# Attention with tokens held by grid columns, half of the keys for the neighbourhood heads, and bias tables stored and read in larger pieces

## The reference

```
h = HybridMixer(x)     # one q/k/v projection; 8 differential heads (each the difference of two softmaxes
                       # over all 512 keys, with a T5 relative bias); 8 neighbourhood heads; output projection
x = LayerNorm(alpha * x + h)
f = PEER(x)            # 8 heads pick 16 of 128*128 single-neuron experts per token
x = LayerNorm(alpha * x + f)
```

```
col_start = jnp.clip(c - NA_WIN_W // 2, 0, GRID_W - NA_WIN_W)
in_win = (c[None, :] >= col_start[:, None]) & (c[None, :] < col_start[:, None] + NA_WIN_W)
bias = jnp.where(in_win[None, None, :, None, :], bias, NEG_INF)
```

## Time and profile before

| | |
|---|---|
| median of 3 runs | 3465.18 us (3463.68 to 3468.54) |
| profiled execution | 3473.33 us, span 3471.5 us |
| mean granted clock of TensorE | 0.964 |
| PE busy | 3242.8 us, 93% of the span |
| DVE busy | 2541.5 us, 73% |
| ACT busy | 1238.2 us, 36% |
| POOL busy | 882.0 us, 25% |

### The profile page before, as it was taken

One profiled execution on the slowest core, in us unless ns is written; L12 is line 12 of the kernel. 1 busy time (PEld: TensorE's weight loads), 2 busy tenths in 40 slices (PEclk: granted clock), 3 DMA queues, 4 the chain that ended last, 5 costly groups with the idle time before them and its releaser, 6 DMA issues. The chain is left out here.

```text
span 3471.5 us, 49403 instructions
## 1 busy us (share of the span) xinstructions
PE 3242.8 (93%) x17110; PEld 2854.6 (82%) x17110; DVE 2541.5 (73%) x5172; ACT 1238.2 (36%) x1716; POOL 882.0 (25%) x624
## 2 busy tenths in 40 slices
PE   6989799899999999999879887998999999999997
PEld 5966589899899999988658665898998999999886
DVE  2166478999688878878721764789996888787787
ACT  2255333344333333333322642333443333333332
POOL 0030001100255545433200200011002555454332
PEclk8989899999999999999989898999999999999999
DMA  7541224445899999989675412244468999998896
GB/s 246 160 113 64 88 85 135 169 181 226 302 356 338 349 328 340 319 308 350 222 229 154 135 39 99 74 146 158 181 236 318 341 362 347 311 343 311 316 350 226
DMA packets 361706, 811.60 MB, mean 234 GB/s; under 512 B 51246, under 2 KB 222766, under 8 KB 327246
## 3 DMA queue, kind: packets, MB, share of 16 engines
q1 hardware_dynamic: 287822, 541.22, 45.5%
q0 software_dynamic: 73728, 268.47, 20.7%
HBM read 718.38 MB, written 99.09 MB: 235 GB/s over the span
## 5 line engine op out<-in xcount | busy, mean ns | idle before, releaser
L221 PE MATMUL o_bank<-v_hi,w_hi 128*128 128x512 f32 x1536 | 599.6, 390 | 10.2 <-DVE w_lo L1526 10.2
L222 PE MATMUL o_bank<-v_lo,w_hi 128*128 128x512 f32 x1536 | 600.6, 391 | 0.0
L223 PE MATMUL o_bank<-v_hi,w_lo 128*128 128x512 f32 x1536 | 600.4, 391 | 0.0
L158 POOL DMA_INDIRECT g_ring<-in_peer_u,g_idx x256 | 363.8, 1421 | 794.0 <-DVE g_ring L168 743.6
L158 POOL DMA_INDIRECT g_ring<-in_peer_v,g_idx x256 | 369.8, 1445 | 508.4 <-DVE x_sb L176 453.9
L221 PE MATMUL h_bank<-x_hi,ws_hi 128*128 128x384 f32 x1152 | 387.1, 336 | 4.5 <-PEq L1194 4.5
L223 PE MATMUL h_bank<-x_hi,ws_lo 128*128 128x384 f32 x1152 | 387.0, 336 | 0.0
L222 PE MATMUL h_bank<-x_lo,ws_hi 128*128 128x384 f32 x1152 | 386.7, 336 | 0.0
L1511 DVE TENSOR_TENSOR v_lo<-v_raw,v_hi 128x2048 fp32r<-128x2048 f32 x128 | 292.9, 2288 | 124.9 <-ACT v_hi L1446 123.0
L168 DVE SCALAR_TENSOR_TENSOR g_ring<-g_ring,x_sb 128x1024 f32<-128x1024 f32 x256 | 306.4, 1222 | 97.8 <-DMA g_ring<-in_peer_u,g_idx 97.3
L176 DVE SCALAR_TENSOR_TENSOR x_sb<-g_ring,g_h,x_sb 128x1024 f32<-128x1024 f32 x256 | 328.4, 1283 | 56.1 <-DMA g_ring<-in_peer_v,g_idx 37.7
(11 more groups left out here) (187 smaller groups left out, 6014.8 us busy)
## 6 DMA issues: line engine op xcount, KB each, us to landing
ws_raw<-in_uT SPq DMA_DIRECT2D x128, 1024.0 KB
v_raw<-in_peer_v SPq DMA_DIRECT2D x128, 1024.0 KB
gates_T<-gate_stage SPq DMA_DIRECT2D x12, 4096.0 KB, 12.6
g_raw<-gates_T SPq DMA_DIRECT2D x128, 384.0 KB
w_raw<-in_w_in SPq DMA_DIRECT2D x24, 1024.0 KB, 7.4
ws_raw<-hidden_T SPq DMA_DIRECT2D x56, 384.0 KB
w_out_half<-in_w_out SPq DMA_DIRECT2D x8, 2048.0 KB, 7.9
ws_raw<-in_peer_wq SPq DMA_DIRECT2D x16, 1024.0 KB
```

The costliest lines, as they stand in the source:

```text
L158: nc.gpsimd.indirect_dma_start(out=tail.ring[n % RING][:, :], out_offset=None, in_=table.rearrange("l e d -> (l e) d"), in_offset=bass.Ind ...
L221: nc.tensor.matmul(out, lh, rh, start=start, stop=False)
L222: nc.tensor.matmul(out, lh, rl, start=False, stop=False)
L223: return nc.tensor.matmul(out, ll, rh, start=False, stop=stop)
```

## The change

The tokens of a tile are now 16 grid columns with all 8 rows of each (`column_tokens`), so the window of a tile's queries lies in 32 columns, 256 keys (`NKEYS`), whose first column depends on the tile (`FIRST_COL`). Neighbourhood heads make, exponentiate, transpose and multiply 256 keys where they did 512. For tiles 1 and 2 the keys begin in the middle of a v tile, so `nv2` is a copy of v shifted by 64 partitions. `x` and the output are loaded and stored in four transfers each.

The bias tables keep their order by rows, and `maxima` reads them with a view that puts columns first (`rearrange("p (r c) -> p c r")`), so that the step between two numbers read is 64 (`tb`) or 32 (`nb`). `tb` has 560 numbers per head and partition where it had 896. The table of the neighbourhood heads is loaded raw (8 x 48 numbers per head) into the buffer of `w_out`, in 8 transfers; GpSimd adds one of three masks and writes the result to `nb`, first for the left edge (8 instructions of 256 numbers), then for the middle and the right edge (8 of 512). SyncE waits for all ten signals (`nb_ready`) before it loads `w_out`.

The 2-D bias is copied to DRAM in 128 rows of 30720 bytes (before: 7680 of 512); the T5 vectors are stored once, in `setup`, from ScalarE's queue. Tail pieces have other slots, the RMS norm has semaphores of its own, and `read_diff` waits for the projection of the tile before (`hid`). In `route` VectorE keeps 3 splits and GpSimd does the other 22, in front of the `place_off` of each head.

```
-TBW = T + (TT - 1) * P
+TC = GW // TT
+TBW = T + (TT - 1) * TC
 DRS = 2 * WIN_H - 1
-RPW = 2 * GW
-NBR = 2 * GR - 2
+RPW = GW
+KC = TC + WIN_W
+NKEYS = KC * GR
+FIRST_COL = (0, TC - WIN_W // 2, 2 * TC - WIN_W // 2, GW - KC)
+EDGE = (0, 1, 1, 2)
+SPAN = KC + TC
+RPL = TC
+RPC = NNH * DRS * RPW + GR * RPW
...
+def column_tokens(t, n):
+
+    return at(t, n * TC * D, [[D, TC], [GW * D, GR], [1, D]])
...
+            act.wait_ge(vec_made, 2)
+            nc.scalar.dma_start(at(t5_scratch, 0, [[NDH * REL, P], [REL, NDH], [1, REL]]),
+                                per["t5_vec"][:, None, :].to_broadcast([P, NDH, REL])).then_inc(t5_stored, 16)
...
-            sp.dma_start(rpb_scratch, at(a["na_rpb"], l * (NNH * DRS * RPW), [[RPW, NNH * DRS], [0, GW], [1, RPW]]))\
+            sp.dma_start(at(rpb_scratch, 0, [[GR * RPC + 1, TC], [RPC + RPW, GR], [1, NNH * DRS * RPW]]),
+                         at(a["na_rpb"], l * (NNH * DRS * RPW), [[0, TC], [0, GR], [1, NNH * DRS * RPW]]))\
                 .then_inc(rpb_copied, 16)
-            sp.dma_start(at(t5_scratch, 0, [[NDH * REL, P], [REL, NDH], [1, REL]]),
-                         per["t5_vec"][:, None, :].to_broadcast([P, NDH, REL])).then_inc(t5_stored, 16)
...
-                    sp.dma_start(tb[:, :, :], at(t5_scratch, P - 1, [[REL - 1, P], [P * REL, NDH], [1, TBW]]))\
-                        .then_inc(tab_in, 16)
-            sp.wait_ge(tab_in, 16)
+                    for h in range(NDH):
+                        src = at(t5_scratch, h * P * REL + (T - 1) - (TT - 1) * TC,
+                                 [[GR * REL - 1, TC], [REL - GW, GR], [1, TBW]])
+                        sp.dma_start(tb[:, h, :], src).then_inc(tab_in, 16)
+            sp.wait_ge(tab_in, 16 * NDH)
...
-        nb = m.sb("na_toeplitz", [P, NNH, NBR, GW])
+        nb = m.sb("na_bias", [P, 3, NNH, GR, KC])
+        nv2 = m.sb("nv_half_shifted", [P, TT - 1, 512])
         wo = m.sb("w_out_half", [P, DC, D // 2])
+        nb_raw = wo[:, :, :].rearrange("p c f -> p (c f)")[:, 0:NNH * GR * SPAN]\
+            .rearrange("p (h r c) -> p h r c", h=NNH, r=GR)
...
-        PE_SLOTS = {"turn_na": 20, "turn_diff": 22, "mul_0": 24, "mul_1": 25, "mul_2": 29, "mul_3": 30}
-        ACT_SLOTS = {"turn_na": 22, "turn_diff": 24}
-        DVE_SLOTS = {"read_diff": 18, "read_na": 20, "gain": 20, "add_0": 28, "add_1": 33, "stats": 33, "norm": 34}
-        POOL_SLOTS = {"read_diff": 18, "stats": 33}
-        SP_SLOTS = {"mul_1": 25}
+        PE_SLOTS = {"turn_na": 20, "turn_diff": 23, "mul_0": 26, "mul_1": 27, "mul_2": 30, "mul_3": 31}
+        ACT_SLOTS = {"turn_na": 22, "turn_diff": 25}
+        DVE_SLOTS = {"read_diff": 18, "read_na": 20, "gain": 21, "add_0": 30, "add_1": 35, "stats": 37, "norm": 39}
+        POOL_SLOTS = {"read_diff": 18, "stats": 37}
+        SP_SLOTS = {"mul_1": 27}
...
+        def chunks(u):
+            return TT if is_diff(u) else NKEYS // P
...
-                for r in range(2):
-
-                    src = at(rpb_scratch, (h * DRS + 1 - r) * GW * RPW + GW - 1,
-                             [[RPW - 1, GW], [GW * RPW, NBR], [1, GW]])
-                    sp.dma_start(nb[r * GW:(r + 1) * GW, h, :, :], src).then_inc(nb_in[h], 16)
+                src = at(rpb_scratch, h * DRS * RPW + (GR - 1) * RPW + RPL - 1, [[RPC, P], [RPW, GR], [1, SPAN]])
+                sp.dma_start(nb_raw[:, h, :, :], src).then_inc(nb_in[h], 16)
+            sp.dma_start(nv2[0:P // 2, :, :], nv[P // 2:P, 0:TT - 1, :]).then_inc(nv2_in, 16)
+            sp.dma_start(nv2[P // 2:P, :, :], nv[0:P // 2, 1:TT, :]).then_inc(nv2_in, 16)
+            sp.wait_ge(nb_ready, NNH + 2)
             load_wo(wo[:, :, :], half(0, 0))
...
-                pool.wait_ge(nb_in[h], 32)
-                nc.gpsimd.tensor_tensor(nb[:, h, :, :], nb[:, h, :, :],
-                                        per["mask"][:, None, :].to_broadcast([P, NBR, GW]), ALU.add)\
-                    .then_inc(nb_ready, 1)
+                pool.wait_ge(nb_in[h], 16)
+                masked(0, slice(h, h + 1), 1).then_inc(nb_ready, 1)
+            for edge in (1, 2):
+                for h in range(0, NNH, 2):
+                    ins = masked(edge, slice(h, h + 2), 2)
+                ins.then_inc(nb_ready, 1)
...
-                    if qt == 0 and not is_diff(u):
-                        dve.wait_ge(nb_ready, h - NDH + 1)
                     if is_diff(u):
-                        bias = tb[:, h, (TT - 1 - qt) * P:(TT - 1 - qt) * P + T]
+                        keys, first = T, (TT - 1 - qt) * TC
+                        bias = tb[:, h, first:first + T].rearrange("p (r c) -> p c r", r=GR)
                     else:
-                        bias = nb[:, h - NDH, GR - 2 - 2 * qt:2 * GR - 2 - 2 * qt, :].rearrange("p r c -> p (r c)")
-                    nc.vector.tensor_tensor_reduce(s[u % PB][:, k, :], S[(before + k) % SB][:, :], bias, -1.0,
+                        dve.wait_ge(nb_ready, h - NDH + 1 if qt == 0 else NNH + EDGE[qt])
+                        keys, bias = NKEYS, nb[:, EDGE[qt], h - NDH, :, :].rearrange("p r c -> p c r")
+                    by_column = lambda t: t.rearrange("p (c r) -> p c r", r=GR)
+                    nc.vector.tensor_tensor_reduce(by_column(s[u % PB][:, k, 0:keys]),
+                                                   by_column(S[(before + k) % SB][:, 0:keys]), bias, -1.0,
...
+                    if qt >= 1:
+                        dve.wait_ge(hid, 2 * qt)
...
-                        q, key = qn[:, (h - NDH) // 2, h % 2, :], nkT[:, (h - NDH) // 2, :]
-                    ins = nc.tensor.matmul(out[:, :], q, key, start=True, stop=True)
+                        first = FIRST_COL[qt] * GR
+                        q, key = qn[:, (h - NDH) // 2, h % 2, :], nkT[:, (h - NDH) // 2, first:first + NKEYS]
+                        out = out[:, 0:NKEYS]
+                    ins = nc.tensor.matmul(out, q, key, start=True, stop=True)
...
-                for k in range(TT):
+                for k in range(chunks(u)):
...
-                v = dv if is_diff(u) else nv
-                for k in range(TT):
+                qt = u // NH
+                v, first = (dv, 0) if is_diff(u) else ((nv, nv2, nv2, nv)[qt], (0, 0, 1, 2)[qt])
+                if v is nv2:
+                    pe.wait_ge(nv2_in, 32)
+                n = chunks(u)
...
-    SPLITS = [("half", "best")] * 2 + [("half", "best", "keys")] * 6
+    FIRST_SPLITS = 3
+    SPLITS = [2, 2, 3, 3, 3, 3, 3, 3]
...
+            def split(n):
+                pool.wait_ge(hi_done, n + 1)
+                pool.wait_ge(lo_done, n)
+                nc.gpsimd.tensor_tensor(wl[n % 2][:, :, :], raw[n % 2][:, :, :],
+                                        wh[n % 2][:, :, :].bitcast(F32), ALU.subtract).then_inc(lo_done, 1)
+
+            n = FIRST_SPLITS
             for j in range(PH):
+                for _ in range(SPLITS[j]):
+                    split(n)
+                    n += 1
...
-            sp.dma_start(out.rearrange("o (t p) d -> p (o t) d", p=P), per["x"][:, :, :]).then_inc(written, 16)
-            sp.wait_ge(written, 16)
+            for tt in range(TT):
+                sp.dma_start(column_tokens(out, tt), per["x"][:, tt, :]).then_inc(written, 16)
+            sp.wait_ge(written, 16 * TT)
```

More of the change, by code:

```diff
@@ L100, in constants @@
     onehot = (np.arange(BUCKETS)[:, None] == bucket[None, :]).astype(np.float32)
-    c = np.arange(GW)
-    start = np.clip(c - WIN_W // 2, 0, GW - WIN_W)
-    inside = (c[None, :] >= start[:, None]) & (c[None, :] < start[:, None] + WIN_W)
-    mask = np.where(inside, 0.0, NEG).astype(np.float32)
-    mask = np.concatenate([mask, mask], axis=0)
+    cq = np.arange(P) // GR
+    mask = []
+    for t in (0, 1, TT - 1):
+        start = np.clip(t * TC + cq - WIN_W // 2, 0, GW - WIN_W)
+        ck = FIRST_COL[t] + np.arange(KC)
+        inside = (ck[None, :] >= start[:, None]) & (ck[None, :] < start[:, None] + WIN_W)
+        mask.append(np.where(inside, 0.0, NEG).astype(np.float32))
+    mask = np.stack(mask, axis=1)
     li = np.array([0.8 - 0.6 * math.exp(-0.3 * l) for l in range(DEPTH)])
@@ L811, in scores @@
                         pe.wait_ge(maxed, before + k - SB + 1)
-                    out = S[(before + k) % SB]
+                    out = S[(before + k) % SB][:, :]
                     if is_diff(u):
@@ L1046, in topk @@
             def topk(j):
-                due = iter(range(3 + sum(len(q) for q in SPLITS[:j]), BLOCKS + 1))
-                def after(step):
-                    if step in SPLITS[j]:
-                        split(next(due))
                 s, best = sc[j], sv[:, j * TT:(j + 1) * TT, :]
@@ L1064, in topk @@
                         halves[:, :, 1, None, 0:width].to_broadcast([P, TT, count, width]), ALU.add))
-                after("half")
                 chain.wait()
@@ L1089, in topk @@
                                                               shf[:, 2, :, :], ALU.mult, ALU.add))
-                after("keys")
                 chain.wait()
```

(2 more changed lines are left out.)

62 lines of the change are left out of this document (38 added, 24 removed).

## The result

The changed kernel takes 3437.03 us (3433.27 to 3442.69, 4 runs) against 3465.57 of the kernel before beside it: a ratio of 0.9917, 95% interval 0.9902 to 0.9933. That is 28.5 us faster where 117 were forecast, and outside the forecast range.

The account below looks back on a forecast made before the run. TensorE bounds the attention, with stalls in projection and routing; projection 39, attention 75, routing 8, start -5 sum to 117 us, so 3473.3 becomes 3356 profiled, 3348 us median; own range 3330 to 3372, wider range 3325 to 3405.

Parts of the forecast that it names:

- The projection: Projection stage: the wait for w_lo goes (17.6 us) and 1.9 us of clock returns, 19.5 us a layer, 39 us.
- beside the first weights, 5 us: Start of the first layer: T5 store beside the first weights costs 4 us, x and output in four transfers 1 us.
- The routing: Routing stage: 22 of 25 splits move from VectorE to GpSimd at 4.5 us each; gain 4.3 us a layer, some 8 us.
- the end is 2.4 us later, not 0.3: End of routing: the last place_off stands behind the last split, making the final wait 4.0 us, 0.3 more than 3.66.
- The attention, a tile: Attention, per tile of 128 queries: halved keys save TensorE 8.6 us, 53 to 44.4; three tiles give 25.7 us a layer.
- So I leave the stall as it is: Attention, per tile: TensorE's stalls, mostly a 9.1 us wait for rowmax over the stage, were taken as unchanged.
- VectorE's excess: Attention, steps 2 to 8: VectorE's work beyond TensorE's, 7 to 8 us, about as before; score banks absorb 3 to 4.
- Strided bias reads: Rival in the attention's maxima: doubled reads cost 0.53 us per 512 elements, leaving 13 us a layer, 3397 us; chance 0.18.
- ScalarE's copy out of a bank: Evidence on strided reads: with step 128 it took 587 ns, dense 586; the prediction therefore took no cost.
- VectorE's own row with a step of 16: Evidence on strided reads: copying 32 elements 16 apart took 182 ns, a dense operation on 64 took 189; left open.
- The first tile: Attention, first tile: a new wait of some 5 us for q parts, gain 6 us up to there and 2 us behind.
- The end of the attention: Last attention tile: norm comes last, so VectorE's chain to the second transposes is 3.8 us shorter per layer.

Follow-up runs that it names:

- t5_late: Changed kernel with the T5 vectors stored in each layer behind the third half block, not once at the start, and the mask loaded ahead of x: 3432.31 us.
- no_reload: Changed kernel without the reload of w_out between the two output halves of tiles 0 to 2, so with another output: 3396.06 us.
- kept_wout_only: Changed kernel with 14 chunks of w_out in SBUF in place of 8, only two loaded again between a tile's halves; all products made: 3398.42 us.
- full_keys_dense_no_reload: Changed kernel with dense bias slices, no reload of w_out between halves, and 512 keys again for the neighbourhood heads: 3402.74 us.
- full_scores: Changed kernel with dense bias slices and no w_out reload between halves, where only the neighbourhood heads' scores matmul has 512 keys again: 3381.98 us.

## Why the prediction was wrong

- **The projection** held in its mechanism: the stall of 17.6 us is gone in both layers, the copy took 16.6 us (12 to 20). The second layer gained 18.1 of 19.5. The term "beside the first weights, 5 us" was too small: 3.9 of start and 5.3 less gain in the first layer, 9.2 us. `t5_late` puts the 5.3 on the store and leaves the 3.9 with `x`.
- **The routing** was right in mechanism, and in size partly by luck: 4.6 and 3.4 us for 4.3. A split on GpSimd takes 4.62 us (4.5), and TensorE waits for none. But the end is 2.4 us later, not 0.3, and 4.9 less 2.4 leaves 2.5 only; the rest was in no term:

```profile
L1180 POOL TENSOR_TENSOR ws_lo<-ws_raw,ws_hi 128x2048 fp32r<-128x2048 f32 x44 | 203.2, 4618 | 242.7 <-ACT ws_hi L1028 242.7
```

- **The attention, a tile**, is where it failed: "TensorE is left with 53 - 8.6 = 44.4 us, stalls included, so it still bounds and the 8.6 us count". The 8.6 us of work were right (some 32 and 35 us at full clock in the two layers, for 34.3 in four tiles). That they count was wrong, for three reasons. First, the reload of `w_out` between `mul_1` and `mul_2` was in no step of the prediction. In the first layer it landed at most 0.4 us late before, hidden by units that the change makes shorter and fewer; now it costs 18 to 19 us a layer in `no_reload`, its slow clock included (`kept_wout_only`: 20 to 22). Second, of the saved work itself only 8 to 15 us a layer reach the end, 19 to 26 less than forecast: in the first layer some 13 are lost to slower matmuls and 14 to idle time, in the second 5 and 11. Third, the strided reads, 7 to 10 us a layer. Together that makes 48 to 53 us a layer, and only 35 to 39 are missing. The rest is a gain that was in no term either: the 16 to 17 us that full_keys_dense_no_reload shows with all keys, of which the forecast had 3.8.
- **"So I leave the stall as it is"** was made from VectorE's excess alone. The waits for `rowmax` fell, 9.1 to 3.7 us; the stall came out at the copy of the turned weights (2.4 to 16.9 us), which stands behind exponents that wait for maxima.
- **Strided bias reads** were the first rival, at 24.5 us a layer for a doubled read (0.53 us). The cost is real, 0.36 us per 512 elements, and on the path it is 7 to 10 us a layer. Taking none from ScalarE's copy out of a bank was the wrong row: it showed another engine and another memory. VectorE's own row with a step of 16 left it open. The rule of the Trainium skill that is named there (SBUF — State Buffer, Specifications) pointed the right way.
- **The first tile** got its new wait for q parts, 0.6 us where 5 were forecast, since TensorE was ready for them at 210.6 us only. With the two costs gone it is ready at 203.6, and the wait is 7.7 us in the first layer, near the forecast. The end of the attention waits 2.4 and 2.3 us for 5.8 and 1.2, so 2.3 us less of the 3.8.

Open stays how the idle time and the clock share the part of the halving that is lost (27 us in the first layer, 17 in the second), since no run held one of them fixed, and what made the gain with all keys.

## What to carry to other kernels

A saving on the bounding engine counts only for as long as everything that hid behind it stays hidden: go through each load that is issued when one piece of work ends and needed when another begins, and compare its time to land with the distance after the change. Look at the granted clock after a saving as well: here the mean over the attention was 0.95 and 0.94 with all keys, and 0.87 and 0.90 with half of them. And price a new access pattern by one small run on the engine and memory that it is for.

## What the runs showed of the hardware that was not expected

- VectorE's add and minimum over 512 floats takes 0.69 us with its SBUF operand at a step of 1 or 2 elements, 0.84 at 3, and 1.04 to 1.14 at 4 to 64.
- 27 us more of TensorE's work in two layers cost 3.7 us (full_scores). The mean granted clock of the attention went from 0.87 to 0.93 in the first layer and stayed at 0.90 in the second.
- A store of 4096 KB from ScalarE's queue took 0.59 us to issue and 15.9 us to land, where SyncE's took 28.41 us to issue behind other transfers.
